# Thirty of 32 experts get 64 rows, with rounded rows and remainders side by side in one stationary block

## The reference, cut to what matters

```python
g_prob = softmax(xt @ w_rg + b_rg); grp = argmax(g_prob)          # 4 groups
e_logits = (xt @ w_re + b_re)[its group]; top_v, top_i = top_k(e_logits, 2)
gate = softmax(top_v) * g_w                                         # 8 experts a group, 32 in all
hdn = silu(xb @ w1[e]) * (xb @ w3[e])                              # 1024 -> 512
y = (hdn @ w2[e]) * w                                               # 512 -> 1024, summed over the two experts
```

## Time and profile before

| | us |
|---|---|
| median of the runs | 3092.04 |
| lowest, highest | 3083.98, 3095.84 |
| profiled execution | 3085.34 |
| its span | 3083.6 |
| TensorE matmul busy | 2996.3 (97%) |
| TensorE weight load busy | 2324.1 (75%) |
| VectorE busy | 2146.3 (70%) |
| ScalarE busy | 1597.3 (52%) |
| GpSimd busy | 369.5 (12%) |

### The profile page before, as it was taken

How to read it: one execution, slowest core, us unless ns; L and a number is a source line. 1 busy time by engine, 2 the same in 40 slices (tenths; PEclk the granted TensorE clock), 3 DMA queues, 4 the chain that set the end, 5 groups by cost and what they waited for, 6 DMA issues and landing times.

```text
span 3083.6 us, 39084 instructions
## 1 busy us (share of the span) xinstructions
PE 2996.3 (97%) x14781; PEld 2324.1 (75%) x14781; DVE 2146.3 (70%) x2336; ACT 1597.3 (52%) x1911; POOL 369.5 (12%) x275
## 2 busy tenths in 40 slices
PE   8999899999999999999999989999999999999998
PEld 7667677777768766677777757888888888788887
DVE  3486888888873376888888865674686638677662
ACT  3573577777764383777777743453322215632211
POOL 0001112222220002122222130010000000000000
PEclk9999999999999999999999999999999999999999
DMA  7303899999972125899999963220332232223222
GB/s 277 120 1 137 298 363 360 365 364 367 359 273 98 49 80 207 331 359 365 368 365 365 368 178 96 56 55 1 123 98 93 96 110 96 89 89 109 82 96 82
DMA packets 174738, 600.50 MB, mean 195 GB/s; under 512 B 25537, under 2 KB 74865, under 8 KB 125203
## 3 DMA queue, kind: packets, MB, share of 16 engines
q1 hardware_dynamic: 140432, 541.22, 49.0%
q0 software_dynamic: 23680, 52.61, 4.8%
q10 hardware_dynamic: 10499, 4.91, 0.6%
HBM read 582.01 MB, written 48.23 MB: 204 GB/s over the span
## 4 chain that ended last, share of the span: by engine, by line
PE 88%; DVE 4%; ACT 2%; DMA 2%; issue 1%; POOL 1%; DVEq 0%; POOLq 0%; ACTq 0%
PE bank L2029 23%; PE bank L2031 23%; PE bank L2030 23%; PE bank L2041 3%; PE bank L2419 2%; PE bank L2720 2%; PE bank L2093 1%; PE bank L2094 1%; PE bank L2036 1%; PE bank L2037 1%; PE bank L2193 1%; PE bank L2459 1%; DMA big<-expert_rows,idx 1%; PE bank L2213 1%; PE bank L2251 0%
## 5 line engine op out<-in xcount | busy, mean ns | idle before, releaser
L3475 DVE TENSOR_TENSOR ring_rounded<-ring,big_rounded 128x2048 fp32r<-128x2048 f32 x252 | 571.2, 2288 | 52.7 <-ACT big_rounded L1439 50.8
L1439 ACT ACTIVATE big_rounded<-ring 128x2048 fp32r<-128x2048 f32 x252 | 479.9, 1917 | 60.8 <-DMA ring<-w_up 29.7
L2030 PE MATMUL bank<-ring_rounded,big_rounded 128*96 128x512 f32 (+1 forms) x1256 | 493.1, 393 | 0.0
L3022 DVE TENSOR_TENSOR ring_rounded<-ring,ring_rounded 128x2048 fp32r<-128x2048 f32 (+2 forms) x118 | 261.4, 2255 | 331.4 <-ACT ring_rounded L1181 331.0
L1181 ACT ACTIVATE ring_rounded<-ring 128x2048 fp32r<-128x2048 f32 (+2 forms) x124 | 226.7, 1876 | 371.8 <-DMA ring<-ffn_w_down 150.8
L2031 PE MATMUL bank<-big_rounded,XH_rounded 128*96 128x512 f32 x992 | 389.8, 393 | 0.0
L3475 DVE TENSOR_TENSOR ring_rounded<-ring,ring_rounded 128x2048 fp32r<-128x2048 f32 x128 | 292.4, 2288 | 87.2 <-ACT ring_rounded L1439 86.8
L1439 ACT ACTIVATE ring_rounded<-ring 128x2048 fp32r<-128x2048 f32 x128 | 244.8, 1916 | 158.6 <-DMA ring<-w_gate 158.4
L2029 PE MATMUL bank<-ring_rounded,big_rounded 128*96 128x512 f32 (+1 forms) x760 | 303.2, 399 | 6.0 <-DVE XH_rounded L3485 5.4
L2031 PE MATMUL bank<-ring_rounded,XH_rounded 128*96 128x512 f32 (+1 forms) x776 | 305.0, 393 | 0.0
L2029 PE MATMUL bank<-XT_rounded,ring_rounded 128*128 128x512 f32 (+1 forms) x792 | 295.8, 374 | 0.4 <-DVE XH_rounded L3075 0.4
(11 more groups left out here) (495 smaller groups left out, 5187.0 us busy)
## 6 DMA issues: line engine op xcount, KB each, us to landing
ring<-w_up SPq DMA_DIRECT2D x128, 1024.0 KB, 7.9
ring<-w_down SPq DMA_DIRECT2D x128, 1024.0 KB, 7.1
ring<-w_gate SPq DMA_DIRECT2D x128, 1024.0 KB, 7.6
ring<-ffn_w_up SPq DMA_DIRECT2D x44, 1024.0 KB, 6.6
ring<-ret_gdn_w_in SPq DMA_DIRECT2D x8, 2048.0 KB, 13.9
ring<-ffn_w_down SPq DMA_DIRECT2D x8, 2048.0 KB, 7.8
expert_rows<-lnp POOLq DMA_DIRECT2D x1, 12288.0 KB, 40.3
ring<-odd_w_qkv SPq DMA_DIRECT2D x6, 2048.0 KB, 8.0
```

What stands on the lines that cost most here:

```text
L1439: act.activation(one_pass(expert_hi(j)), expert_raw(j), ACT.Copy).then_inc(signal("half_rounded").sem, 1)
L2030: pe.matmul(dst, x_hi, y_lo, start=False, stop=False)
L3022: dve.tensor_tensor(one_pass(w), w, parts(hi(c)[:, ks, :]), ALU.subtract).then_inc(split[c.pair], 1)
L3475: dve.tensor_tensor(one_pass(expert_raw(j)), expert_raw(j), parts(expert_hi(j)), ALU.subtract).then_inc(signal("half_split").sem, 1)
```

## The change

- `NARROW = 64`: experts at places 2 to 31 have 64 rows, those at places 0 and 1 keep 96.
- The stationary block of gate and up holds 64 rounded columns and 64 remainder columns side by side (`XN`). `up_narrow` multiplies it with the rounded weights and with their remainders, 2 matmuls in place of 3, and gets 128 rows: the parts of the rounded rows above, those of the remainders below.
- The two halves have to be added. For gate, ScalarE copies bank 2 (`gate_parts`), TensorE multiplies with `both`, a 128 x 128 matrix of four 64 x 64 identities, in full float32 into bank 7 (`gate_sum`), and the activation reads bank 7. The up part stays unsummed; the hidden product is made on 128 partitions, and the transposes become full float32 matmuls with `both`, which add the halves.
- On ScalarE the activation stands behind the rounding of gate 0 of the next expert. On VectorE the row remainders stand ahead of the hidden product.
- Expert order: the fullest of experts 1 to 31 changes places with expert 1. VectorE works out the order and the tables in `slots_and_scores` (23 dependent operations in place of 4, and the order in SBUF); SP reads the expert of each place from SBUF (`value_load`) ahead of its weight transfers, and waits once for the table.
- Gathers, scatters and copies of places 2 to 31 name 64 rows.

The core of the diff:

```diff
         M = carve([("XE", (2, D)), ("XET", (2, KD, P)), ("hid", (2, D_EXPERT)), ("YE", (2, D))], 8192)
+        M["XN"] = M["XET"]
         M["XET"] = M["XET"][:, :, :, 0:CAP]
         M["XET_lo"] = XH[:, 0:2, :].rearrange("p b (k c) -> p b k c", k=KD)[:, :, :, 0:CAP]
         M["HT_lo"] = XH[:, 2:4, 0:KE * P].rearrange("p b (k c) -> p b k c", k=KE)[:, :, :, 0:CAP]
-        M["HT"] = XH[:, 2:4, KE * P:2 * KE * P].rearrange("p b (k c) -> p b k c", k=KE)[:, :, :, 0:CAP]
+        M["HN"] = XH[:, 2:4, KE * P:2 * KE * P].rearrange("p b (k c) -> p b k c", k=KE)
+        M["HT"] = M["HN"][:, :, :, 0:CAP]
+        M["both"] = big[:, 15360:15360 + P]
...
+        def slots_of(e):
+
+            return CAP if isinstance(e, int) and e < WIDE_EXPERTS else NARROW
+
+        def rows_of(bank, n, c):
+
+            return bank[:, 0:n * CAP].rearrange("p (k c) -> p k c", k=n)[:, :, 0:c]
+
+        def turned_hidden(e):
+
+            c = slots_of(e)
+            return psum[4][:, 0:KE * c].rearrange("p (k c) -> p k c", k=KE)
+
+        def whole_rows(e, half):
+
+            return M["XET"][:, half] if slots_of(e) == CAP else M["XN"][:, half, :, 0:NARROW]
+
+        def rest_rows(e, half):
+
+            return M["XET_lo"][:, half] if slots_of(e) == CAP else M["XN"][:, half, :, NARROW:P]
+
+        def whole_hidden(e, half):
+
+            return M["HT"][:, half] if slots_of(e) == CAP else M["HN"][:, half, :, 0:NARROW]
+
+        def rest_hidden(e, half):
+
+            return M["HT_lo"][:, half] if slots_of(e) == CAP else M["HN"][:, half, :, NARROW:P]
+
...
                 def next_gate_up(e):
 
+                    w = expert_at(e + 1)
                     for (b, js), n in zip(((2, GATE), (3, UP)), halves_used(l, e)):
                         sp.wait_ge(signal("half_used").sem, n)
-                        expert_half(e + 1, js[0])
+                        expert_half(w, js[0])
                         sp.wait_ge(full[b], e + (base[b] + 1))
-                        expert_half(e + 1, js[1])
+                        expert_half(w, js[1])
 
                 def next_down(e):
 
+                    w = expert_at(e)
                     sp.wait_ge(signal("half_used").sem, halves_used(l, e - 1)[2] if isinstance(e, int) else halves_used(l, e)[1] + 1)
-                    expert_half(e, DOWN[0])
+                    expert_half(w, DOWN[0])
                     sp.wait_ge(full[6], e + base[6])
-                    expert_half(e, DOWN[1])
+                    expert_half(w, DOWN[1])
 
...
+                sp.wait_ge(signal("used_ready").sem, l + 1)
                 next_gate_up(0)
...
                     pool.indirect_dma_start(
-                        M["XE"][0:CAP, e % 2, :], None, expert_rows, bass.IndirectOffsetOnAxis(ap=used[0:CAP, e:e + 1], axis=0),
+                        M["XE"][0:slots_of(e), e % 2, :], None, expert_rows, bass.IndirectOffsetOnAxis(ap=used[0:slots_of(e), e:e + 1], axis=0),
                         bounds_check=EXPERTS * CAP - 1, oob_is_err=False,
...
+                def gate_parts(e, half):
+
+                    wait_use(full, 2, e)
+                    act.activation(M["hid"][:, half, :], psum[2][:, :], ACT.Copy).then_inc(drained[2], 1)
 
                 def silu(e, half):
-                    wait_use(full, 2, e)
-                    act.activation(M["hid"][0:CAP, half, :], psum[2][0:CAP, :], ACT.Silu).then_inc(drained[2], 1)
+                    if slots_of(e) == CAP:
+                        wait_use(full, 2, e)
+                        act.activation(M["hid"][0:CAP, half, :], psum[2][0:CAP, :], ACT.Silu).then_inc(drained[2], 1)
+                    else:
+                        act.wait_ge(full[7], nth_sum(l, e))
+                        act.activation(M["hid"][:, half, :], psum[7][:, :], ACT.Silu).then_inc(drained[7], 1)
 
...
-                    silu(e, half)
+                    gate_parts(e, half)
                     if down:
                         round_half(e - 1, DOWN[1])
                     if not last:
                         round_half(e + 1, GATE[0])
+                    silu(e, half)
+                    if not last:
                         rows_T(e + 1, 1 - half)
...
+                def up_narrow(e, half, early=False):
+
+                    for b in range(2):
+                        wait_use(drained, b, e, 1)
+                    for js, b in ((GATE, 2), (UP, 3)):
+                        wait_use(drained, b, e)
+                        for i, j in enumerate(js):
+                            pe.wait_ge(signal("half_rounded").sem, nth_split(l, e, j, early))
+                            for kk in range(4):
+                                pe.matmul(psum[b][:, :], one_pass(M["XN"][:, half, 4 * i + kk, :]), one_pass(expert_hi(j)[:, kk, :]), start=(i + kk == 0), stop=False)
+                            pe.wait_ge(signal("half_split").sem, nth_split(l, e, j, early))
+                            for kk in range(4):
+                                ins = pe.matmul(psum[b][:, :], one_pass(M["XN"][:, half, 4 * i + kk, :]), one_pass(expert_raw(j)[:, kk, :]), start=False, stop=(4 * i + kk == KD - 1))
+                            if i == 0:
+                                ins.then_inc(signal("half_used").sem, 1)
+                        ins.then_inc(full[b], 1)
+
+                def gate_sum(e, half):
+
+                    wait_use(drained, 2, e, 1)
+                    pe.wait_ge(drained[7], nth_sum(l, e) - 1)
+                    pe.matmul(psum[7][:, :], M["both"], M["hid"][:, half, :], start=True, stop=True).then_inc(full[7], 1)
+
                 def hidden_T(e, half):
                     wait_use(drained, 3, e, 1)
                     wait_use(drained, 4, e)
                     for kk in range(KE):
+                        if slots_of(e) == NARROW:
+                            ins = pe.matmul(turned_hidden(e)[:, kk, :], M["hid"][:, half, :].rearrange("c (h p k) -> c h k p", h=2, k=2)[:, kk // 2, kk % 2, :],
+                                            M["both"][:, 0:NARROW], start=True, stop=True)
+                            continue
...
-                                ins = product(psum[b][0:CAP, :], M["HT"][:, half, kk, :], M["HT_lo"][:, half, kk, :],
+                                ins = product(psum[b][0:slots_of(e), :], whole_hidden(e, half)[:, kk, :], rest_hidden(e, half)[:, kk, :],
...
-                    up(e, half, early=early)
+                    up_narrow(e, half, early=early)
+                    gate_sum(e, half)
                     if not last:
...
+                dve.scalar_tensor_tensor(key, count, -float(EXPERTS), k("iota"), ALU.mult, ALU.add).then_inc(dve_done.sem, 1)
+                done()
+                dve.tensor_reduce(n_most, key[:, 1:EXPERTS], AX_X, ALU.min).then_inc(dve_done.sem, 1)
+                done()
+                dve.tensor_scalar(most, key, n_most, None, ALU.is_equal).then_inc(dve_done.sem, 1)
+                done()
+                dve.tensor_tensor(tmp, most, k("iota"), ALU.mult).then_inc(dve_done.sem, 1)
+                done()
+                dve.tensor_reduce(which, tmp, AX_X, ALU.add).then_inc(dve_done.sem, 1)
+                done()
+                dve.tensor_scalar(back, which, -1.0, 1.0, ALU.mult, ALU.add).then_inc(dve_done.sem, 1)
+                done()
...
+                dve.tensor_copy(used[:, 1:2], row_most).then_inc(signal("used_ready").sem, 1)
+                dve.wait_ge(signal("used_ready").sem, signal("used_ready").next(dve))
+                dve.scalar_tensor_tensor(tmp, most, -float(CAP - NARROW), count, ALU.mult, ALU.add).then_inc(drained[u.bank], 1)
                 dve.wait_ge(drained[u.bank], u.n + 1)
-                dve.scalar_tensor_tensor(used, R["row"], -float(NO_ROW), k("row_or_none"), ALU.mult, ALU.add).then_inc(
-                    signal("used_ready").sem, 1)
-                dve.wait_ge(signal("used_ready").sem, signal("used_ready").next(dve))
-                dve.tensor_scalar(gsum[:, 0:1], gsum[:, 0:1], -float(CAP), 0.0, ALU.add, ALU.max).then_inc(dve_done.sem, 1)
-                dve.wait_ge(dve_done.sem, dve_done.next(dve))
...
-                    wait_use(drained, 2, e)
-                    h = M["hid"][0:CAP, half, :]
-                    dve.tensor_tensor(h, h, psum[3][0:CAP, :], ALU.mult).then_inc(drained[3], 1)
+                    c = P
+                    if slots_of(e) == CAP:
+                        c = CAP
+                        wait_use(drained, 2, e)
+                    else:
+                        dve.wait_ge(drained[7], nth_sum(l, e))
+                    h = M["hid"][0:c, half, :]
+                    dve.tensor_tensor(h, h, psum[3][0:c, :], ALU.mult).then_inc(drained[3], 1)
 
...
+                    for c in range(0, P, NARROW):
+                        dve.tensor_tensor(M["both"][:, c:c + NARROW], ident[:, 0:NARROW], ident[:, NARROW:P], ALU.add).then_inc(signal("both_ready").sem, 1)
+                        dve.wait_ge(signal("both_ready").sem, signal("both_ready").next(dve))
```

(3 more changed lines are left out.)

66 lines of the change are left out of this document (53 added, 13 removed).

## The result

The changed kernel takes 2994.1 us in the median of four runs (2992.8 to 2996.3) against 3089.4 for the kernel before beside it: a ratio of 0.969, 95% interval 0.967 to 0.971, so some 95 us faster. The forecast was 3063, its range ended at 3030. The sign was right; the size was three times too small.

What follows compares the result with a forecast made beforehand. The prediction took TensorE to bound the kernel, with DMA 3% behind. Steady stages -25.2, tail -4.4 and layer starts +0.8 summed to -28.8 us, giving a median of 3063 us, range 3030 to 3090.

Steps and rivals of the forecast that it cites:

- TensorE's new work: Each stage of experts 2 to 31: TensorE's work falls to 15.8 us, 2.2 less than before.
- I count nothing; fewer places can only gain: GpSimd's scatter and gather naming 64 places instead of 96: same bytes moved, so no saving counted.
- the steady term: Stages from up(3) to up(31), both layers: period 17.95 to 17.5 us, 0.45 saved in each, 25.2 us in all.
- DMA share 0.97 taken as 17.4 us of work in 17.95: Steady stages: DMA needs 17.4 us of each 17.95 us period, so only 0.5 us can be freed.
- Transfers already queue 2.6 us, so the engines hardly lack work: Steady-stage weight transfers: they already queue 2.6 us, the argument against a deeper queue running faster.
- the faster queue: Rival: in steady stages a deeper queue lifts DMA to 410 GB/s, period about 16.1 us, 2985 us total; chance 0.11.
- The start of a layer: VectorE's longer slot table costs 4.0 us, stage 2 gains 3.2 over both layers: net 0.8 us lost.
- The tail and the SP loads: Layer's end: TensorE alone, 4.4 us saved in all. SP's register loads hide; uncovered, up to 1.4 us in landing.
- The chain through the later activation: Rival: steady stages, the activation's new transfer wait makes the chain exceed 17.95 us; 3116 us total; chance 0.08.
- The clock: Rival: TensorE's idle in steady stages lowers its granted clock, mean period 18.4 us, 3114 us total; chance 0.05.
- DMA already full: Rival: steady period stays 17.8 to 17.95 us, only tail and start remain, 3080 to 3089 us; chance 0.21.
- the late path: Rival: an expert beyond the two wide ones exceeds 64 rows, float32 path runs all experts, 2.8 ms more; chance 0.01.

Runs made afterwards that it cites:

- a_plus8: The changed kernel with 8 matmuls more in each narrow gate and up product: 3062.5 us, ratio 0.992 to the kernel before.
- b_drop8_spread: b_drop8 with each expert's rows spread over its 96 places by a permuted table of constants: 2981.7 us, ratio 0.965 to the kernel before.
- b_spread: The kernel before, all its matmuls kept, with the rows spread over the 96 places: 3086.7 us, ratio 0.999.
- a_g96: The changed kernel with gathers and scatters of experts 2 to 31 naming 96 places again: 3060.9 us, ratio 0.991 to the kernel before.
- b_drop8: The kernel before with 8 gate and up matmuls fewer per expert from expert 2 on, 96 places in order: 3037.4 us, ratio 0.984.
- a_g96_spread: The changed kernel with 96-place gathers and scatters, each narrow expert's rows spread over its first 64 places: 3023.5 us, ratio 0.979 to the kernel before.
- b_g64: The kernel before with 64 places in the gathers and scatters from expert 2 on: 3085.9 us, ratio 0.999.
- a_direct: The changed kernel fetching the weights of expert e at place e, without SyncE's register loads: 2991.0 us, ratio 0.968 to the kernel before.
- a_drop8: The changed kernel with 16 instead of 24 down matmuls for experts 2 to 31: 3001.2 us, ratio 0.972 to the kernel before.
- a_packed: The changed kernel with an expert's some 32 rows in places 0 to 15 and 32 to 47 of 64: 3031.3 us, ratio 0.982 to the kernel before.

## Why the prediction was wrong

- **TensorE's new work** (15.8 us): right. 15.82 in the timeline, 15.5 by a_plus8; gate sum 0.85 for 0.9, merging transposes 0.95 for 1.0.
- **"I count nothing; fewer places can only gain"**: the step that failed. With 96 places kept, the stage is 17.51 us and the kernel 3061, which is the forecast. The 64 places gave 67 us of the 95 (1.30 us a stage, 56 times, is 73). In the sum it is the steady term: (17.95 - 16.21) x 56 = 97 us where 25.2 stood. I had reasoned from bytes, which stay, and from empty places that move nothing; what counted is where the real rows lie among the places (56 us in b_drop8_spread), most likely by which DMA engines carry them.
- **DMA share 0.97 taken as 17.4 us of work in 17.95**: failed. From 420 to 840 us the share was 1.01, 0.99 and 0.98 at 403, 376 and 364 GB/s, and 0.96 at 364 in b_spread. So that a_g96 comes out at the forecast's 17.5 us is luck: b_drop8, with 96 places and the old order of work, has 17.23, and 96 places in another order have 16.85 (a_g96_spread) and 16.23 (b_drop8_spread). The bound of 16.9 us that I had from the stretch with 0.94 was too high for the same reason.
- **"Transfers already queue 2.6 us, so the engines hardly lack work"**, the argument against the faster queue: failed. b_g64 and b_spread shorten that queue by 2 us at the same rate. That the faster queue's number came does not make its reason right: the longest landings go with the low rate of a_g96. And the 4.9 us taken for a lone transfer are those of six issued at 377.1, 380.2, 382.8, 385.5, 389.4 and 392.1 us, so they overlapped in pairs.
- **The start of a layer** (0.8 us lost): half right. TensorE's first row transposes came 4.6 us later in layer 0, not 3.3. Of this 0.8 us lay ahead of the table (it began at 308.42, not at 307.66), 3.7 are the longer way from its first operation to VectorE's copy (6.2 us for 2.55), and 0.2 is ScalarE's first copy, which stood behind its exponentials and ends last (L1523 ends the 4.74 us gap). The clock fell with it. By the sixth stage all was given back in layer 0 (403.20), with three narrow gate and up products ahead of it; moving the operations shows some 3 us a layer in the total, within the noise.
- **The tail and the SP loads**: the loads cost nothing that a_direct can show (2991.0). The tail was not isolated.
- **The chain through the later activation** (rival): it exists, small. In a_g96 TensorE's matmuls wait 14.4 us in 24 stages for the hidden product, in b_drop8, with the old chain, 0.5 us once; their stages are 17.51 and 17.23 though TensorE has less to do in a_g96, and this chain is the likeliest cause, not tested by itself. In a_drop8 it ends all of TensorE's waits. It never decided above 17.95.
- **The clock** (rival): 1.00 in the steady stages of both layers. At the start it was 0.74 from 310 to 330 us, around the end of the 4.74 us gap, where the kernel before has 0.99, and 0.83 in the 20 us from the second layer's first transposes on, where it has 1.00. In a_drop8 it may be what ate the gain.
- **DMA already full** and the late path: did not happen.

## What to carry to other kernels

Don't read a DMA share near 1 as a limit: change the demand or the load and look at the rate and the landings. Where a gather or scatter fills few of its places, the position of the full ones counts, most likely because it decides which DMA engines carry them; permuting the table of places costs nothing and was worth 56 us where the transfers were the bound, none where they were not. When one change lightens two resources that run side by side, its two parts are not additive: 50 us for eight matmuls less alone, none for the places alone, 95 for both parts of the change together.

## What was unexpected of the hardware

- Sustained 403 to 405 GB/s for 420 us into a core whose engines are all busy.
- 96 places and 64 places of an indirect DMA seem to be dealt to the engines by different rules: in order is the worst of three orders tried for 96 and the second best of four for 64. The rules are inferred from times, and others may fit; no view names the engine of a packet. a_g96_spread's 16.85 us need no further price for the 32 places more: by the rules its fullest engine has some 4.2 rows, as a_packed's has 4.0 at 16.90 us.
- With 1.85 us of TensorE's work a stage taken away, a_drop8 gained nothing and was 9 us slower than the changed kernel beside it, at a mean granted clock 0.015 lower; not explained.
